# Dilated attention in a four-part decoder trunk: both heads' value products on column halves of the array, scores emptied as a pair, projection tiles emptied in halves

## What is computed

```python
DIL_GROUPS = ((128, 1), (512, 4), (2048, 16))
DIL_HEADS = 4
...
    scale = Dh ** -0.5
    k_groups = [k[:, :, g] for g in range(G)]
    v_groups = [v[:, :, g] for g in range(G)]
...
        for g in range(G):
            idx = t[:, None] - offsets[g][None, :]
            valid = idx >= 0
            idx = jnp.maximum(idx, 0)
            kg = k_groups[g][:, idx]
            vg = v_groups[g][:, idx]
            logits = jnp.einsum('bqhd,bqkhd->bhqk', qb[:, :, g], kg, preferred_element_type=jnp.float32) * scale
            logits = logits + group_bias[g][None, :, None, :].astype(jnp.float32)
            logits = jnp.where(valid[None, None], logits, NEG_INF)
            lse = jax.nn.logsumexp(logits, axis=-1)
            p = jnp.exp(logits - lse[..., None])
            outs.append(jnp.einsum('bhqk,bqkhd->bqhd', p.astype(v.dtype), vg))
            lses.append(lse)
        wts = jax.nn.softmax(jnp.stack(lses, axis=0), axis=0)
        return jnp.einsum('gbhq,gbqhd->bqhd', wts.astype(v.dtype), jnp.stack(outs, axis=0))
```

## Time and profile before

| | us |
|---|---|
| median of 3 runs | 3041.12 (3038.4 to 3057.72) |
| the profiled execution | 3036.58 |
| its span, first to last instruction | 3034.8 |
| PE busy in the span | 2867.4 (94%) |
| PE weight loads busy | 2330.8 (77%) |
| DVE, ACT, POOL busy | 1147.3, 848.9, 922.2 |

### The profile page before, as it was taken

How to read it: one execution, slowest core, us unless ns; L and a number is a source line. 1 busy time by engine, 2 the same in 40 slices (tenths; PEclk the granted TensorE clock), 3 DMA queues, 4 the chain that set the end, 5 groups by cost and what they waited for, 6 DMA issues and landing times.

```text
span 3034.8 us, 36334 instructions
## 1 busy us (share of the span) xinstructions
PE 2867.4 (94%) x13684; PEld 2330.8 (77%) x13684; DVE 1147.3 (38%) x1835; ACT 848.9 (28%) x1481; POOL 922.2 (30%) x610
## 2 busy tenths in 40 slices
PE   8998888989999999999999999877899999999998
PEld 5786777867888888886788777767688888888867
DVE  3425777324222222225433334577332222222254
ACT  3305766432100001114311222666511110001250
POOL 2331144432333333334222213122333333333432
PEclk9999999999999999999999999799999999999999
DMA  4455522211111111111242213553111111111112
GB/s 156 150 171 174 135 54 63 84 42 35 49 49 48 48 48 48 48 63 35 83 170 80 37 36 38 120 120 106 57 46 46 48 48 48 48 48 48 63 35 77
DMA packets 80706, 220.42 MB, mean 73 GB/s; under 512 B 24803, under 2 KB 28387, under 8 KB 80279
## 3 DMA queue, kind: packets, MB, share of 16 engines
q1 hardware_dynamic: 69800, 178.77, 21.0%
q10 hardware_dynamic: 10784, 40.01, 3.4%
HBM read 185.22 MB, written 37.20 MB: 73 GB/s over the span
## 4 chain that ended last, share of the span: by engine, by line
PE 84%; DVE 8%; issue 2%; ACT 2%; SPq 2%; DMA 2%; POOL 1%; DVEq 0%; ACTq 0%; POOLq 0%
PE ACC L1242 70%; PE OP L1444 3%; PE TR L1419 3%; PE ACC L1405 3%; SPq L951 1%; DVE PT L2140 1%; DVE XL L1938 1%; PE OP L1314 1%; PE OP L1434 1%; DVE H L1958 1%; DVE T L1955 1%; ACT PT L1726 1%; DMA RAW<-in_w 1%; DVE PB L2119 1%; PE ACC L1382 1%
## 5 line engine op out<-in xcount | busy, mean ns | idle before, releaser
L1049 POOL CAST WH<-RAW 128x1024 fp32r<-128x1024 f32 x188 | 197.8, 1052 | 1422.5 <-PE ACC L1242 1394.4
L1242 PE MATMUL ACC<-XH,WH 128*128 128x512 f32 x1792 | 572.0, 400 | 33.8 <-DVE XL L1938 26.8
L1242 PE MATMUL ACC<-XL,WH 128*128 128x512 f32 x1792 | 554.6, 391 | 0.0
L1242 PE MATMUL ACC<-XH,WL 128*128 128x512 f32 x1792 | 554.3, 391 | 0.0
L1051 POOL TENSOR_TENSOR WL<-RAW,WH 128x1024 fp32r<-128x1024 f32 x188 | 453.3, 2411 | 22.2 <-POOL WH L1049 0.7
L1242 PEld LDWEIGHTS ACC<-XH,WH 128*128 128x128 f32 x1792 | 336.2, 189 | 132.0 <-issue 51.2
L1242 PEld LDWEIGHTS ACC<-XL,WH 128*128 128x128 f32 x1792 | 337.9, 189 | 71.2
L1242 PEld LDWEIGHTS ACC<-XH,WL 128*128 128x128 f32 x1792 | 337.8, 189 | 71.2
L1687 ACT ACTIVATE HH<-T 128x1024 fp32r<-128x1024 f32 x64 | 67.9, 1061 | 1149.7 <-DVE T L1980 1149.7
L1987 DVE TENSOR_TENSOR M<-M,ACC 128x1024 f32<-128x1024 f32 x128 | 156.3, 1221 | 481.7 <-PE ACC L1242 479.5
L1242 PE MATMUL ACC<-HH,WH 128*128 128x512 f32 x1024 | 316.6, 390 | 3.3 <-DVE M L1987 3.1
(11 more groups left out here) (215 smaller groups left out, 3415.5 us busy)
## 6 DMA issues: line engine op xcount, KB each, us to landing
RAW<-in_w SPq DMA_DIRECT2D x203, 512.0 KB, 3.5
QK<-y_odds SPq DMA_DIRECT2D x56, 256.0 KB, 5.8
QK<-y_foxs SPq DMA_DIRECT2D x48, 256.0 KB, 5.3
y_foxs<-HALVES ACTq DMA_DIRECT2D x8, 1024.0 KB, 5.3
BIAS<-y_f SPq DMA_DIRECT2D x8, 512.0 KB, 7.0
y_kv<-HALVES ACTq DMA_DIRECT2D x8, 512.0 KB, 3.2
H<-in_xT ACTq DMA_DIRECT2D x8, 512.0 KB, 6.4
y_h<-H ACTq DMA_DIRECT2D x8, 512.0 KB, 2.6
```

The source lines that it names most:

```text
L1049: nc.gpsimd.tensor_copy(WH[:, slot], RAW[:, slot]).then_inc(s_whi, 1)
L1242: mm = nc.tensor.matmul(acc[:, h * HALF:(h + 1) * HALF], w(k), x[:, k, h * HALF:(h + 1) * HALF], start=first and k == k0 and w is ws and x ...
```

## The change

Four edits, all in the dilated jobs:

- `values` runs once for both heads of a chunk pair. Each head multiplies its own 64 value columns and writes its own 64 rows of one bank, head 0 and head 1 in turn. Both heads' halves share a bank, and the next pair of halves takes the other. `DILATED_LAG` is 3, and only a chunk of head 1 sets it off, so both come at step 4c+6.
- ACT copies both heads' rows from OP to DU at once.
- DVE's `scores` and ACT's `probabilities` run for both heads at the even step.
- The last k-block of a projection tile does columns 0 to 511 first (`s_th`), then 512 to 1023 (`s_tile`). DVE empties in two instructions (`s_dh`, then `s_evD`), and the next tile's first k-block follows in the same halves.

```diff
-TURN_LAG, VALUE_LAG, DILATED_LAG = 2, 5, 4
+TURN_LAG, VALUE_LAG, DILATED_LAG = 2, 5, 3
...
+            earlier_half = lambda bank: next((x for x in reversed(halves) if x.bank == bank), None)
...
-                n["whole"] += kind in DILATED
-                x.prior = halves[-1] if halves else None
+                n["whole"] += e * (kind in DILATED)
+                bank = halves[-1].bank if halves else 1
+                x.bank = bank if e == 1 and in_pairs else 1 - bank
+                x.last = earlier_half(x.bank)
...
-            if ended and ended is ended.chunk.tasks[1]:
+            if ended and ended is ended.chunk.tasks[1] and (ended.e == 1 or ended.kind not in DILATED):
...
+        def scored(st):
+            t = st.logits
+            if not t or t.kind in DILATED and t.e:
+                return []
+            return t.job.tasks[2 * t.i:2 * t.i + 2] if t.kind in DILATED else [t]
...
-                    if c.opens and c.half.prior:
-                        taken(pe, c.half.prior.prior)
+                    if c.opens:
+                        taken(pe, c.half.last)
                     order = sorted(c.keys, key=lambda x: x[1] - x[2])
                     if j.kind in DILATED:
+                        both = [x for x in j.chunks if x.c == c.c]
                         for n, (k, c0, c1) in enumerate(order):
-                            mm = nc.tensor.matmul(OP[:, c.half.no % 2, col + c0:col + c1], VF[:, j.slot, k],
-                                                  PF[:, c.buf, k - c.k0, c0:c1], start=c.opens and n == 0,
-                                                  stop=c.closes and n == len(order) - 1, skip_group_check=True)
-                        mm.then_inc(s_pv, 1)
+                            for x in both:
+                                rows = rows_of_head(x.e)
+                                mm = nc.tensor.matmul(OP[rows, c.half.bank, col + c0:col + c1], VF[:, j.slot, k, rows],
+                                                      PF[:, x.buf, k - c.k0, c0:c1], start=c.opens and n == 0,
+                                                      stop=c.closes and n == len(order) - 1, skip_group_check=True)
+                                if n == len(order) - 1:
+                                    mm.then_inc(s_pv, 1)
...
+                    n = mix.index(u)
+
+                    def passes(halves):
+                        for m, (w, x) in enumerate(((WH, X1H), (WH, X1L), (WL, X1H))):
+                            for h in halves:
+                                cols = slice(h * HALF, (h + 1) * HALF)
+                                mm = nc.tensor.matmul(ACC[:, t.pair, cols], w[:, slot, k * P:(k + 1) * P], x[:, k, cols],
+                                                      start=k == 0 and m == 0, stop=k == DC - 1 and m == 2)
+                        return mm
+
                     if k == 0:
                         pe.wait_ge(s_split, u.no + 1)
+                        if n:
+                            pe.wait_ge(s_dh, n)
+                        else:
+                            evacuated([t], 0)
+                        passes([0])
                         evacuated([t], 0)
-                    mm = three_pass(ACC[:, t.pair], k, k + 1, lambda k: WH[:, slot, k * P:(k + 1) * P],
-                                    lambda k: WL[:, slot, k * P:(k + 1) * P], X1H, X1L, k == 0, k == DC - 1)
-                    if k == DC - 1:
-                        mm.then_inc(s_tile, 1)
+                        passes([1])
+                    elif k == DC - 1:
+                        passes([0]).then_inc(s_th, 1)
+                        passes([1]).then_inc(s_tile, 1)
+                    else:
+                        passes([0, 1])
...
-                        dst, src = by_token(h, DU[h.job.pair][rows, DILATED.index(h.job.kind)], OP[rows, h.no % 2])
+                        dst, src = by_token(h, DU[h.job.pair][:, DILATED.index(h.job.kind)], OP[:, h.bank])
...
-                    if st.logits:
-                        probabilities(st.logits)
+                    for t in scored(st):
+                        probabilities(t)
...
                 t = ts[0]
-                need(dve, s_tile, [x.no + 1 for x in ts], it)
+                if t.mixed:
+                    dve.wait_ge(s_th, t.idx - 2)
+                else:
+                    need(dve, s_tile, [x.no + 1 for x in ts], it)
...
-                        dst = dst.rearrange("p (r j) -> p j r", r=NB)
-                        src, r = (x.rearrange("p (j r) -> p j r", r=NB) for x in (src, r))
-                    V_.tensor_tensor(dst, src, r, ALU.mult).then_inc(s_evD, 1)
+                        dst = dst.rearrange("p (r h j) -> p h j r", r=NB, h=2)
+                        src, r = (x.rearrange("p (h j r) -> p h j r", h=2, r=NB) for x in (src, r))
+                    else:
+                        dst, src, r = (x.rearrange("p (h j) -> p h j", h=2) for x in (dst, src, r))
+                    if not t.mixed:
+                        V_.tensor_tensor(dst, src, r, ALU.mult).then_inc(s_evD, 1)
+                        return
+                    V_.tensor_tensor(dst[:, 0], src[:, 0], r[:, 0], ALU.mult).then_inc(s_dh, 1)
+                    dve.wait_ge(s_tile, t.no + 1)
+                    V_.tensor_tensor(dst[:, 1], src[:, 1], r[:, 1], ALU.mult).then_inc(s_evD, 1)
...
-                    if st.logits:
-                        scores(st.logits)
+                    for t in scored(st):
+                        scores(t)
```

More of the change, by code:

```diff
@@ L646, in program @@
         s_qh = sem("s_qh")
+        s_th = sem("s_th")
+        s_dh = sem("s_dh")
         s_ql = sem("s_ql")
@@ L1443, in values @@
                                 v, pt = VCS[:, c.e * P:(c.e + 1) * P], PTC[:, c.buf, hl, c0:c1]
-                            mm = nc.tensor.matmul(OP[:, c.half.no % 2, col + c0:col + c1], v, pt,
+                            mm = nc.tensor.matmul(OP[:, c.half.bank, col + c0:col + c1], v, pt,
                                                   start=c.opens and n == 0 and hl == 0,
@@ L1702, in correction @@
                     wait(act, s_o, h.cor - 1)
-                    nc.scalar.activation(CORR[rows], OP[other, h.no % 2], ACT.Copy).then_inc(s_cor, 1)
+                    nc.scalar.activation(CORR[rows], OP[other, h.bank], ACT.Copy).then_inc(s_cor, 1)
                 def copy_v(j):
@@ L2173, in outputs @@
                         dve.wait_ge(s_ops, j.ops[1])
-                    V_.tensor_tensor(dst, OP[rows, h.no % 2], CORR[rows], ALU.add).then_inc(s_o, 1)
+                    V_.tensor_tensor(dst, OP[rows, h.bank], CORR[rows], ALU.add).then_inc(s_o, 1)
                     if h.groups:
```

## The result

The changed kernel takes 3023.3 us (median of 10 runs, 3010.75 to 3036.63), the kernel before, run beside it on the same chip, 3043.28 us (10 runs, 3038.4 to 3057.92): a ratio of 0.9923, 95% interval 0.9901 to 0.9946. The medians are 20 us apart; the ratio is worth 23 us (16 to 30). A second series of the same pair, in five rounds, gave 0.9925 (0.9899 to 0.9952). The profiled execution took 3023.48 us.

What follows compares the result with a forecast made beforehand. PE, busy 94% of 3034.8 us, was taken as the bound. Terms -9.8 + 2.0 - 9.4 - 4.6 - 2.2 = -24.0 us took 3036.58 to 3012.6; the median's 4.5 us offset gave 3017, range 3004 to 3032.

Steps and rivals of the forecast that it cites:

- the halves don't take turns: First rival, dilated value products: column halves take turns and save 0, total -14.2 us, 3027 us; chance 0.18.
- the waits came back: Second rival, PE in the dilated stretch: values wait for DVE instead, clock still falls, -10 us, 3031 us; chance 0.10.
- loads are not exposed: Third rival, value products: they take turns with weight loads exposed, +6.0 us in all, 3047 us; chance 0.05.
- the fourth: Fourth rival, dilated jobs: products fully side by side, no wait left, one more copy off ACT's chain, 3007 us; chance 0.12.
- The value products: Five dilated jobs beside projections: both heads' products on column halves, partly overlapped in staggered order, save 9.8 us.
- The change of shape: PE's array around dilated value blocks: one more change of shape a block, 20 blocks x 0.1 = +2.0 us.
- The loads: Weight loads of the value products: they hide behind running matmuls, though the skill's row-group rule says they would be exposed.
- PE's waits: PE waiting for DVE at projection tiles' ends: of 14.9 us 5.5 stay, 3.75 and 1.75, so -9.4 us.
- the walk: Step-by-step timing of PE and DVE at a job's first, second and third projection tiles, giving the waits left.
- T-0.49: DVE's predicted start on half 0, with T the end of the projection tile's last matmul; halves end T+0.41 and T+1.31.
- The clock: Dilated stretch: half clock put down to waits of about 2 us; most given back without them, -4.6 us.
- The last job: Last dilated job, without projections: two fewer DU copies on ACT's chain, products hidden behind ACT, -2.2 us.

Runs made afterwards that it cites:

- lag4: The changed kernel with DILATED_LAG put back to 4, so both heads' values stand one step later: stretch 240.7 us, run 3019.79 us, ratio 0.9925.
- copy_between: The changed kernel with DVE making task 7's copy between the two emptying halves at a job's second tile: stretch 238.6 us, run 3016.85 us.
- only_columns: The kernel before with only the paired column-half value products and shared DU copy; scores and emptying as before: stretch 257.0 us, run 3045.73 us.
- third_before: The kernel before, unaltered, profiled a third time: stretch 271.4 us, run 3058.45 us.
- after_timed: The changed kernel, unaltered, timed in rounds against the kernel before: stretch 242.7 us, run 3018.48 us, ratio 0.9925.
- no_columns: The changed kernel with value products, banks, lag and copies of before; paired scores and half emptying stay: stretch 248.4 us, run 3037.52 us.
- head_after_head: The changed kernel with all of head 0's products of a block ahead of head 1's: stretch 245.6 us, run 3015.02 us.

## Why the prediction was right, and which of its terms were not

3017 us was forecast, 3023.3 measured, inside the forecast's own range of 3010 to 3024; the difference to before, 24.0 forecast, is 20 by the medians and 23 by the ratio. Of the rivals, the halves don't take turns, the waits came back in part only, and loads are not exposed; the fourth had the products right and the waits wrong. But two errors met in the forecast, the value products and the clock beyond the stretch. They cancel, so that the total came out is in part luck.

- **The value products: the step that was mis-sized, -7.8 with the change of shape against -12.7.** The forecast walked through the products in a staggered order, on the argument that head 1's first record can start only with head 0's second. The starts above are 6 to 7 ns apart. Less the 0.09 us of the change of shape, a d1 block takes 0.93 us where 1.08 was worked out, a d4 block 0.71 (0.87), a d16 block 0.50 (0.55). And the base was low: 27.2 us came from blocks entered from a projection; the block of head 0, entered from scores, takes 0.1 us more (0.98 for 0.87), 20 times, and the pair keeps less of it. With that the whole base is 29.2 us.
- **The change of shape: right.** From the last value record to the transposes 0.20 us passed, 0.11 before: 0.09 more, 20 times, +1.8 for +2.0. lag4 bears the price out from another side: 1.8 us for 18 blocks.
- **The loads: right.** A half's six loads (6 x 0.137 = 0.82 us) and its six records (0.88 at the old pace) lie together within a block of 1.02 us, so they overlap. The rule that the prediction weighed (the Trainium skill, "TensorE: Matmul & The Clock Gate", Part 3: Packing small matmuls — row/col tiling), that a load overlaps matmuls in flight only where the row group differs, does not hold here: all loads use all 128 rows, and still hide. The trace decides against that sentence of the part for half loads too; why they hide, no run here shows.
- **PE's waits: right in place and nearly in size.** 3.8 us of the values where 3.75 was worked out, 2.3 of the value tile's transposes for 1.75 (five waits over the whole stretch, four of them, 1.7, up to the last projection tile), none for the tile. The times of the walk (T-0.49, T+0.41, T+1.73 for the copy's end) stand in the timeline as T-0.49, T+0.42, T+1.74. Of 14.9 us 6.1 are left, -8.8 for -9.4; up to the last projection tile it is 5.5 of 14.6. copy_between shows the cause, since moving that one copy takes the larger wait away.
- **The clock: right in size in the stretch, its cause not shown, wrong beyond it.** In the stretch no half clock in any of three profiles, against 10 to 17 us in three of before, worth 5 to 9 us; -4.6 was forecast. The forecast put the half clock down to the waits of about 2 us, but only_columns kept all five and had none, so their length alone doesn't decide; the ten profiles without waits of that length had none behind a wait either. Beyond the stretch the sum took the rest of the program to keep its clock. In the profiled execution the sparse jobs ran at 0.81 for 0.89. Over three profiles each they took 193.2, 191.7 and 197.3 us before, 203.6, 200.2 and 196.4 after. Ahead of the stretch, in code that nothing precedes but itself, the time at half clock ran from 20 to 58 us in the runs here, so a good part of this is drawn anew at each execution. Whether the change also makes the draw behind it worse, as 194.1 against 200.1 on average suggests, isn't settled: the two sets of three overlap (third_before 197.3, after_timed 196.4), and the instructions there are the same, but all eleven profiles with a part of the change lean that way. Over all runs whose clock is on record (17 of each) the means are 3044.8 and 3022.1 us, 22.7 apart; along lines fitted through time against each run's mean clock they stand 24.5 apart at a clock of 0.98, where after_timed's theory had 27. So some 4 us of the 27.1 that came off the stretch are missing from the mean; runs that spread by 24 to 26 us don't tell how much of that is the change's own.
- **The last job: the size right, the mechanism not; luck.** From the last projection matmul to the last dilated scores 15.0 us before (1909.28 to 1924.27) and 13.1 after (1887.77 to 1900.87): -1.9 for -2.2. But the forecast left two copies DU on the chain with the products hidden behind ACT. After, ACT has left the chain between 1888 and 1901 us, and the products stand on it:

```profile
1896.26 0.66 PE OP L1450 x8
1896.92 0.37 PE TR L1432 x2
...
1898.32 0.41 DVE PF L2175 x2
```

  only_columns, with two copies left on its chain as forecast, needs 14.7, and no_columns, with all 24 copies, 14.3. So the shared copies with the shorter products gave 0.3 us by themselves; the rest needs the other edits beside them.

The stretch's sum at full clock: products and shape -11.5 and waits -9.1, both up to the last projection tile, and last job -1.9 is -22.5; measured -22.0. With the clock's -5.1, 27.1 came off the stretch, and 20 were left in the run's median (23 by the ratio).

only_columns tells what the forecast's arithmetic leaves out: the terms are not independent. A product made shorter ahead of a wait reaches that wait sooner, so 12.7 us of shorter blocks were worth 7.7 us alone and 5.7 behind the other edits, the last job's part included.

## What to carry to other kernels

Products that use half of the array's columns are worth pairing, and the two sides should alternate in the program: that order was worth 2.9 us here against the same products side after side, nearly all of it in blocks with more than two products a side. Where an engine's queue ends a wait, lay out by hand what stands behind it on that engine: the sums of the waits left came out within 0.6 us that way, and moving one copy between two halves of a long instruction took 4 us off the stretch, though the run's time does not show it. An edit of 20 us in a program of 3000 is judged by its own stretch, at a stated clock, since the clock of untouched code moved by as much from one execution to the next.

## What the runs showed of the hardware that was not expected

- Two fp32 matmuls on different column halves start 5 to 8 ns apart and keep the pace of one; a block of six pairs of records took 1.02 us, and one head's three products alone 0.87 to 0.98.
- Matmuls don't always start in program order: one for the free column half started ahead of three earlier records of the busy half, and no further, in every block of head_after_head.
- Waits of up to 2.1 us do not always lower the clock: only_columns kept five of them and had a granted clock of 1.00 over its 257.0 us, where three profiles of before had 10 to 17 us at half clock.
- The same instructions took 1651.5 us (head_after_head) to 1670.6 us (only_columns) ahead of the stretch, with 20.5 us at half clock in the first and 58.0 in the last.
